# A first MLP whose up half is also made of seven products, with the modulation vectors of the later layers summed earlier in the kernel

## The reference

```
cs = silu(c)                                # one vector of 1024
mod = cs @ ada_w[layer] + ada_b[layer]      # six vectors of 1024 per layer; two more for k and v
layer 0:  y = mlstm_mixer(x*(1+sc_m)+sh_m)  # q, k, v, o projections, recurrence over 8 chunks, output projection
          h = LN(a*x + (1+g_m)*y)
          u = h*(1+sc_f)+sh_f
          h = LN(a*h + (1+g_f) * (square(relu(u @ w_up)) @ w_down))     # w_up 1024x4096
k, v   =  (h*(1+kv_scale)+kv_shift) @ w_kv
layer 1:  windowed attention with its own q, then the same MLP with its own weights
```

## Time and profile before

| | |
|---|---|
| median of 3 runs | 2147.69 us (2147.02 to 2148.5) |
| the profiled execution: its own time, its span | 2148.5 us, 2146.8 us |
| TensorE busy in the span | 2100.7 us (98%), 9816 matmuls |
| DVE, ACT, POOL busy | 1502.8 us (70%), 882.8 us (41%), 270.6 us (13%) |
| granted TensorE clock | 0.997 of full |
| memory read / written | 225.29 MB / 15.76 MB |

### The profile page before, as it was taken

How to read it: one execution, slowest core, us unless ns; L and a number is a source line. 1 busy time by engine, 2 the same in 40 slices (tenths; PEclk the granted TensorE clock), 3 DMA queues, 4 the chain that set the end, 5 groups by cost and what they waited for, 6 DMA issues and landing times.

```text
span 2146.8 us, 28666 instructions
## 1 busy us (share of the span) xinstructions
PE 2100.7 (98%) x9816; PEld 1702.2 (79%) x9816; DVE 1502.8 (70%) x2343; ACT 882.8 (41%) x1529; POOL 270.6 (13%) x248
## 2 busy tenths in 40 slices
PE   6999999999999999999999999999999999999998
PEld 5888888878888888888888777678787888888886
DVE  7423666678676676776768665767788788778878
ACT  4201454162234233342337455655434434534552
POOL 0000220010010110110100023232000011011034
PEclk9999999999999999999999999999999999999999
DMA  7434643303424224224121210211345433533531
GB/s 298 137 102 126 124 94 139 126 20 120 126 69 137 97 79 137 78 83 147 34 98 72 79 30 11 79 58 42 124 182 185 162 131 137 205 114 121 195 137 79
DMA packets 77315, 242.16 MB, mean 113 GB/s; under 512 B 8417, under 2 KB 8593, under 8 KB 73649
## 3 DMA queue, kind: packets, MB, share of 16 engines
q1 hardware_dynamic: 69376, 219.18, 30.1%
q0 software_dynamic: 5088, 17.48, 3.7%
q10 hardware_dynamic: 2768, 4.41, 0.5%
HBM read 225.29 MB, written 15.76 MB: 112 GB/s over the span
## 4 chain that ended last, share of the span: by engine, by line
PE 84%; DVE 7%; DMA 4%; ACT 3%; issue 2%; POOL 1%; SPq 0%; DVEq 0%; ACTq 0%; POOLq 0%
PE ps L2670 25%; PE ps L2672 25%; PE ps L2671 25%; DMA stage<-in_stream 3%; PE ps L3135 1%; PE ps L3165 1%; PE ps L3149 1%; DVE wlo L1609 1%; ACT whi L964 1%; PE ps L2914 1%; PE ps L2773 1%; PE ps L2899 1%; DMA early_place<-in_early 1%; PE ps L2903 1%; DVE stats L1918 1%
## 5 line engine op out<-in xcount | busy, mean ns | idle before, releaser
L2672 PE MATMUL ps<-uhi,wlo 128*128 128x512 f32 x760 | 296.4, 390 | 0.0
L2670 PE MATMUL ps<-whi,uhi 128*128 128x512 f32 x704 | 287.6, 408 | 0.2 <-ACT resid L1309 0.2
L2670 PE MATMUL ps<-uhi,whi 128*128 128x512 f32 x704 | 276.3, 392 | 5.9 <-DVE wlo L1609 3.2
L2672 PE MATMUL ps<-whi,ulo 128*128 128x512 f32 x704 | 275.4, 391 | 0.0
L2671 PE MATMUL ps<-wlo,uhi 128*128 128x512 f32 x704 | 274.8, 390 | 0.0
L2671 PE MATMUL ps<-ulo,whi 128*128 128x512 f32 x704 | 274.8, 390 | 0.0
L2672 PEld LDWEIGHTS ps<-uhi,wlo 128*128 128x128 f32 x760 | 143.1, 188 | 29.8
L2670 PEld LDWEIGHTS ps<-uhi,whi 128*128 128x128 f32 x704 | 132.6, 188 | 37.0 <-DVE wlo L1609 4.6
L2670 PEld LDWEIGHTS ps<-whi,uhi 128*128 128x128 f32 x704 | 132.5, 188 | 36.6 <-issue 10.0
L2672 PEld LDWEIGHTS ps<-whi,ulo 128*128 128x128 f32 x704 | 132.2, 188 | 28.9
L2671 PEld LDWEIGHTS ps<-ulo,whi 128*128 128x128 f32 x704 | 132.5, 188 | 27.2
(11 more groups left out here) (437 smaller groups left out, 4614.6 us busy)
## 6 DMA issues: line engine op xcount, KB each, us to landing
stage<-in_stream SPq DMA_DIRECT2D x248, 512.0 KB, 3.6
hlo<-ulo_dram SPq DMA_DIRECT2D x28, 1024.0 KB, 4.8
ulo<-ulo_dram SPq DMA_DIRECT2D x20, 1024.0 KB, 5.3
w_whole<-in_stream SPq DMA_DIRECT2D x14, 512.0 KB, 5.2
aux<-in_early SPq DMA_DIRECT2D x8, 512.0 KB, 7.5
early_place<-in_early SPq DMA_DIRECT2D x8, 512.0 KB, 14.2
resid<-in_xt SPq DMA_DIRECT2D x8, 512.0 KB, 15.7
resid<-in_x POOLq DMA_DIRECT2D x8, 512.0 KB, 9.7
```

The costliest lines, as they stand in the source:

```text
L2670: pe.matmul(dst, left_hi, right_hi, start=start, stop=False, skip_group_check=more)
L2672: return pe.matmul(dst, left_lo, right_hi, start=False, stop=stop, skip_group_check=more)
```

## The change

1. The middle chunks and the last chunk of the first MLP are made by the same code as those of the second: `both_chunk` replaces `seven_chunk`, `mlp_through(m)` runs either MLP. The sums of quarters of `u`, the stored low parts and the loads back are now made in both. The part `+ ln_b` of the residual, which DVE added in the first MLP together with the scaling, is added by POOL beside the last chunk, for all eight tiles in both MLPs.
2. The seven vectors that were summed in the first MLP move. SH_F0 and SC_F0 and SH_KV (24 blocks) now all lie behind query and key blocks 7 to 13. In the value projection stand SC_KV, SH_M1, SC_M1 and G_M1 (32 blocks, through `stage`, summed in `gate_row`) and, one block per tile, SH_F1 and SC_F1 (16 blocks, through a third place, `scratch`, with queue entries of their own between the `stage` loads on SP). G_F1 is summed beside the second half of the output gate and the output projection. All are summed over partitions by `sum_vector`; `quarters` are gone.
3. In the plain first chunk of each MLP the up weights 2 and 3 are loaded and split first and the down weights after them, each at a later group than before.
4. Small moves: rotary angles and three modulations go from the end of the first MLP's loop to the first tiles of the output projection's second half; `cstate` is copied at the first chunk of the recurrence and no longer cleared; in the attention DVE makes the totals of a pair before the affine of a residual tile.

```diff
+BESIDE_QK = {7: [(SH_F0, 0, 3)], 8: [(SH_F0, 3, 6)], 9: [(SH_F0, 6, 8)], 10: [(SC_F0, 0, 4)], 11: [(SC_F0, 4, 8)],
+             12: [(SH_KV, 0, 4)], 13: [(SH_KV, 4, 8)]}
+BESIDE_V = {t: (v, 2 * n, 2 * n + 2) for first, v in ((1, SC_KV), (5, SH_M1), (9, SC_M1)) for n, t in
+            enumerate(range(first, first + 4))}
+BESIDE_V.update({13: (G_M1, 0, 3), 14: (G_M1, 3, 6), 15: (G_M1, 6, 8)})
...
-CHUNK_LOADS = [4, 5, 2, 3, 6, 7, 8, 9]
+CHUNK_LOADS = [2, 3, 4, 5, 6, 7]
+LOADS_AT = {2: (2,), 3: (3, 4), 4: (5,), 5: (6,), 6: (7,)}
...
-    mlp = "A" * 8 + "D" * 16 + ("A" * 8 + "D" * 28) * len(SEVEN) + "A" * 8 + "D" * 16
+    both = "A" * 6 + "D" * 6 + "A" * 2
+    mlp = "A" * 8 + "D" * 16 + (both + "D" * 28) * len(SEVEN) + both + "D" * 16
...
+            def load_side(n):
+
+                if n:
+                    sp.wait_ge(side_used, n)
+                else:
+                    sp.wait_ge(gate_m, 6)
+                sp.dma_start(scratch[:].rearrange("p a n -> p (a n)"), stream[SIDE_BASE + n]).then_inc(side_in, 16)
+
+            load_pairs(2, IN_V, 0)
+            load_side(0)
+            tile = 1
+            for n in range(IN_V, AFTER_V):
+                load_one(n)
+                while tile < 2 * T and n + 1 >= LOADED_THROUGH[tile - 1]:
+                    load_side(tile)
+                    tile += 1
...
-            for t in range(T):
-                adas(SC_F0, range(t, t + 1))
-                if t == T - 1:
+            for tile in range(2 * T):
+                nh, t = divmod(tile, T)
+                if tile == T - 1:
                     preps(14, 15)
-                evac_v(0, t)
-            for t in range(T):
-                evac_v(1, t)
-                adas(SH_KV, range(t, t + 1))
...
+                evac_v(nh, t)
+                for vec in {0: (SC_F0,), 2: (SH_KV,), 6: (SC_KV,), 9: (SH_F1,), 10: (SH_M1,), 14: (SC_M1,)}.get(tile, ()):
+                    take_mod(vec)
+                ada(SIDE[nh], t)
+                if tile in BESIDE_V:
+                    adas(*BESIDE_V[tile])
+                if tile in (T + 1, T + 2):
+                    preps(7 + tile)
...
-            with v.Fori(0, len(SEVEN)) as i:
-                seven_chunk(chunk_start(FIRST["mlp0"], 1), W_MLP0 + 8, 0, i, 16, True)
...
+            def mlp_through(m, tail, between=None):
+
+                mlp_chunk(m)
+                with v.Fori(0, len(SEVEN)) as i:
+                    both_chunk(m, both_start(FIRST[MLP[m]], 1), 0, i)
+                both_chunk(m, both_start(FIRST[MLP[m]], CHUNKS - 1), len(SEVEN), 0, last=True)
+                if between:
+                    between()
+                last_downs(m, tail)
...
-                    if nh == 1 and t == 0:
-                        sum_vector(SC_F0)
+                    for vec in {1: (SH_KV,), 5: (SC_KV,), 8: (SH_F1,), 9: (SH_M1,), 13: (SC_M1,)}.get(T * nh + t, ()):
+                        sum_vector(vec)
...
+                if more:
+                    totals(2 * p + 2)
                 if p >= T:
                     affine_kv(p - T)
                 if more:
-                    totals(2 * p + 2)
                     totals(2 * p + 3)
```

More of the change, by code:

```diff
@@ L218, in query_groups @@
+MLP = ("mlp0", "mlp1")
 def query_groups():
@@ L1593, in scale, with adas, take_mod @@
+                ins.then_inc(used, 1)
+            def adas(vec, first, end):
+                for k in range(first, end):
+                    ada(vec, k)
+            def take_mod(vec):
+                v.wait_ge(sum_done, SUM_NUMBER[vec] + 1)
+                dst = mods[:, vec, :]
+                v.tensor_tensor(dst, ps[:, SUM_BANK.get(vec, M), 0:K], dst, ALU.add).then_inc(sum_read, 1)
             def scale(n, w, i=0, per=0):
```

1624 lines of the change are left out of this document (692 added, 932 removed).

## The result

The changed kernel takes 2183.86 us (median of 4 runs, 2182.52 to 2187.14), the kernel before 2148.1 us beside it (4 runs, 2147.02 to 2149.89): a ratio of 1.0168, 95% interval 1.015 to 1.0186. It is slower by 36 us where 8 us less were predicted. The profiled execution took 2184.47 us, its span 2182.6, at a granted clock of 0.981 (before 0.997).

What follows compares the result with a forecast made beforehand. TensorE, busy 98% of the span, was taken as the bound. Span 2146.8 − 37.5 (gains less sums) + 26.3 (value projection waits) + 3.0 (rest) = 2138.6, plus 0.9 gives 2139.5 us; whole range 2124 to 2152.

Steps and rivals of the forecast that it cites:

- The middle chunks: First MLP, six middle chunks: would take 460.68 us as in the second MLP, against 498.53, so −37.85 us.
- C: Rival, chance 0.05: first MLP's seven-product up half gains only half, DVE slowed by something only that MLP has; 2158 us.
- the second MLP's chunk 0: Up weights 2 and 3 loaded ahead of down weights end the 2.75 us wait for a low part there.
- two places of `stage`: Value projection: one load's round trip sets the pace, 5.15 us for two loads, 48 loads at 2.575 us.
- the side place itself is never late: Value projection: the third place, for one block per tile, needs one load per tile and causes no wait.
- Step 4 of the value projection: Followed load by load: tile 15 copied at 249.8 with 3.6 us flights, 255.3 with mean 4.0; taken as +26.3 us.
- a neighbour costs a load little more than the neighbour's own data: Value projection loads, from the Trainium skill: 3.2 us for 512 KB, a neighbour adding only its 1.2 us of data.
- Rival B: Chance 0.2: value projection flights lengthen to 5.2 us, 45 us lost, 2158 us; decides from 34.5 us of waits.
- The rest: Recurrence's first chunk with late weights 18 and 19, +1.5 us; angles and weights 96 and 97, +1.5; together bounds 0 and 6.
- Ring banks hide up to two groups: Reason given for the bounds 0 and 6 us on the recurrence's first chunk and the angles and late weights.
- POOL's eight additions lie beside 168 up passes: First MLP's last chunk: additions lie beside TensorE's work; 24 fewer passes and one 0.4 us wait give −5.0 us.
- Attention: Totals ahead of two residual-tile instructions shorten the 3.13 us wait for POOL's `probs`: −2.4 us, bounds 0 and −3.1.

Runs made afterwards that it cites:

- Experiment 2: Changed kernel with POOL's broadcast rows stored so that each partition's transfer is one 2 KB piece, not four of 512 bytes; span 2178.1 us against 2182.6.
- experiment 7: Changed kernel with at most two blocks a value tile, 2 KB broadcast pieces, POOL's additions in two parts, and attention totals back behind the residual tile; 2172.96 us, ratio 1.0111.
- experiment 8: Experiment 7 with one block per recurrence chunk ahead of the first state update, weight 18 split later, POOL's second half earlier in the first MLP; 2156.03 us, ratio 1.0039.
- experiment 10: Experiment 8 with G_F1 moved to the output projection's end and first up groups, G_F0 in its place, weights 18 and 19 split later; 2151.06 us, ratio 1.0016.
- Experiment 3: Changed kernel with POOL's additions of `ln_b` to tiles 4 to 7 put behind the last chunk's up half in both MLPs; span 2172.1 us against 2182.6.
- Experiment 6: Changed kernel with the attention's totals back behind the two instructions on the residual tile, as before the change; span 2179.7 us against 2182.6.
- experiment 4: Changed kernel with 40 extra matmuls into a spare bank, filling TensorE's wait ahead of the sum of SH_KV; span 2181.1 us against 2182.6.
- experiment 11: Experiment 10 with G_F1 partly one block at a time over four up groups, and recurrence blocks and weights 20 and 21 reordered; 2150.9 us, ratio 1.0013.

## Why the prediction was wrong, step by step

The profiled span is 44.0 us above the 2138.6 of the sum: 24.9 ahead of the first MLP and 19.1 behind.

**Right.** The middle chunks: −39.2 against −37.85, and C (half the gain) is refuted. The pace of the matmuls and the second MLP as nearest row held; so did the second MLP's chunk 0 (−3.7 against −2.75; rather more). The first MLP's gave only 0.3 of its 1.5: a new wait of 2.0 us for a low part (`ulo`) stands ahead of chunk 1's first matmul, where the stretches of the earlier trace rows begin, so they don't hold it as the prediction says. That the value projection would be paced by two places of `stage` held: two thirds of DVE's idle time there end with transfers. Of the earlier trace rows it is the first block's place, not the second's, that comes round at 595.77 and 600.89; the 5.15 us are right. One term was small and wrong, "the side place itself is never late": DVE waited for it 3.05 and 1.07 us.

**Step 4 of the value projection, "a mean of 4.0 us" of flight: mis-sized, 9.7 us.** Tile 15 came at 265.0, not 255.3; tile 0 at 154.8, not at 148.5 to 149.5, so more than half of the error stood there already. The 47 loads into `stage` issued from 112 to 262 us took 4.59 us in the mean. Four of them took 8 to 9 us beside POOL's broadcasts; without these four the mean is 4.21. The prediction's own two points (3.6 us gives 249.8, 4.0 gives 255.3), carried on to 4.59, give 263.4, an estimate: 8 of the 9.7 us, so the rule of the two places held and its input was too small. The argument that a neighbour costs a load little more than the neighbour's own data failed beside the broadcasts. Rival B named the right quantity and the wrong neighbour (`w_whole`, 5.2 us), and its condition, flights of 4.5 us or more, was met: 36.0 us were lost against its border of 34.5. Experiment 2 gives back some 4 us by the size of the pieces alone. The last 2 us are not settled; the low clock behind the sum at 95 us, which half of the profiles don't have, may be in them.

**"The rest" (+3.0): mis-sized, 15.2 us, the largest miss.** I followed the recurrence's first chunk with one late weight and priced the output stages at 1.5 us. They lost 8.3 and 13.3 us, of which 3.4 are the two sums. In the recurrence even one place too early for a block delays the state's update: experiments 7 and 8 differ in little else, and by 16 us there. In the output stages G_F1's blocks were to lie beside other work of DVE, and TensorE waited for `qk` and `acc` (2.4 and 1.95 us) and for two low parts (1.2 and 1.8 us); moved away (experiment 10) most of this went. "Ring banks hide up to two groups" was the assumption that failed.

**"POOL's eight additions lie beside 168 up passes": failed, 14.8 us.** 8.3 in the first MLP (+3.3 against −5.0), 6.5 in the second, for which I had no term at all, though the diff changes both. I asked only whether TensorE covers POOL; the one disturbed was DVE, which feeds TensorE. The rows for it stood in the trace before (shown above: 2.83 us beside POOL's four, 1.21 behind them). Experiment 3: −10.5 us, all of the second MLP's 6.5. The 4.3 that stay are in the first, with the two waits behind POOL's second half. The prediction had said that a loss of more than 5 us in another stage would make it wrong in a way that no rival names; this came true in the output stages and in the second MLP's last chunk.

**Attention (−2.4): the sign failed, 7.4 us.** The wait shrank from 3.13 to 1.66 us, and POOL's earlier start ran into DVE's additions. Experiment 6 brings the stretch back to 322.88; the span fell by 2.9.

**The clock: no term.** I priced a wait at its length. The excess of slow matmuls grew by some 18 us over the whole kernel. It can't be added to the terms above, since it lies within them, and where DVE waits for loads it is hidden (experiment 4: some 2 us at tile 2, none at tile 15).

The direction, then, hangs on more than one step: with the changes of 3 and 6 made (10.5 and 2.9 us of the span) the kernel would, by this sum, still be at about 2170. The vectors, 56 blocks and seven sums, put the start of the first MLP's chunk 1 off by 65.8 us in the changed order, and by 43.5 and 45.0 in experiments 10 and 11, the best that I found; what stands behind gives back 30.0 us in the changed kernel and 44 to 45.5 in those two. Their medians are 0.16 and 0.13% above the old time, and neither interval reaches down to 1 (the executions profiled were among the faster ones). So no order that I tried beats the kernel before. Whether a better one is left, I can't say.

## What to carry to other kernels

Work that is moved into idle time has to be followed on the engine it moves to, at each place: the same blocks in the same stage cost some 16 us more or less by where they stood around one update. Before two engines are said to work side by side, look at a row in which they do, and ask who waits for the one that is slowed. And price a row of loads by the flights seen beside the neighbours that it will have, the broadcasts too, not by the median of the page.

## What the hardware showed that I had not expected

- DVE and POOL: an addition of 128 x 1024 with both operands in the core's memory takes 1.21 us alone and 2.5 to 3.4 beside POOL's, POOL's 2.4 and 3.2. With one operand in PSUM (512 columns) it is 0.68 in both cases.
- Broadcasts of 256 KB in pieces of 512 bytes take 6 to 10 us and hold up 512 KB loads beside them to 7 to 10 us (3.5 to 3.6 alone); in pieces of 2 KB 5.1 to 6.7, and the loads 5.3 to 6.6. A load of 64 KB beside them took 7.3 (1.85 alone).
- The clock stood at 1.2 GHz behind a wait of 9.8 us, and sometimes it falls without one: behind the same 1.8 us of 16 one-column matmuls it was 0.59 to 0.80 over four us in five profiles and 1.00 in seven.
